# The first routing step handed to the gather in two halves of eight expert numbers

## What is computed

```python
s1 = jnp.einsum('chk,nk->chn', q[..., :128], keys_1)
s2 = jnp.einsum('chk,nk->chn', q[..., 128:], keys_2)
v1, i1 = lax.top_k(s1, 16)
v2, i2 = lax.top_k(s2, 16)
cand = v1[..., :, None] + v2[..., None, :]
cand_idx = i1[..., :, None] * 128 + i2[..., None, :]
top_s, pos = lax.top_k(cand, 16)
experts = take_along_axis(cand_idx, pos)
gate = softmax(top_s)
u, v = expert_u[experts], expert_v[experts]
act = gelu(einsum('chkd,cd->chk', u, h))
out = einsum('chk,chkd->cd', gate * act, v)
```

## Time and profile before

| | us |
|---|---|
| three timed runs | 2411.83, 2418.49, 2420.32; median 2418.49 |
| profiled execution, its own time | 2412.99 |
| its span in the trace | 2411.3 |
| first gather issued at | 920.23 |
| last gather issued at | 2384.3 |

### The profile page before, as it was taken

The page is one execution under the profiler, slowest core; times in us unless marked ns, Lnnn a source line. Parts: engine busy times, 40 slices in busy tenths (PEclk is TensorE's granted clock), DMA queues, the critical chain, the costliest instruction groups (busy, mean ns, idle before and its releaser), DMA issues.

```text
span 2411.3 us, 26498 instructions
## 1 busy us (share of the span) xinstructions
PE 2082.3 (86%) x8832; PEld 1483.9 (62%) x8832; DVE 1679.4 (70%) x3760; ACT 861.5 (36%) x2094; POOL 634.9 (26%) x606
## 2 busy tenths in 40 slices
PE   7999998899999998999986878787788878777776
PEld 3444787788888887877765666676644423322322
DVE  5563645476657737999998999876676666676654
ACT  2321345421103213423326446356643333342332
POOL 2100000000110002333344334344444443444442
PEclk9999998999999999999997989899799999999999
DMA  8631120266774348999999999999999999999997
GB/s 350 197 121 55 34 71 1 105 225 228 259 282 147 133 157 326 412 417 415 418 416 420 407 379 402 399 398 420 420 420 421 421 421 422 419 421 419 421 422 292
DMA packets 131790, 754.31 MB, mean 313 GB/s; under 512 B 14544, under 2 KB 14672, under 8 KB 65616
## 3 DMA queue, kind: packets, MB, share of 16 engines
q0 software_dynamic: 87456, 588.90, 60.0%
q1 hardware_dynamic: 44208, 163.84, 18.7%
HBM read 750.59 MB, written 2.10 MB: 312 GB/s over the span
## 4 chain that ended last, share of the span: by engine, by line
PE 43%; DMA 31%; DVE 16%; ACT 5%; issue 3%; POOL 0%; DVEq 0%; SPq 0%; ACTq 0%; POOLq 0%
PE PS L603 41%; DMA arena<-experts_dram,ecur 25%; DVE arena L2622 5%; DVE arena L1891 4%; DVE h_all L1891 2%; DMA ring<-down_dram 2%; PE PS L1149 2%; DVE ring L1891 1%; DMA ring<-up_dram 1%; DVE arena L1885 1%; ACT L1761 1%; ACT arena L1765 1%; ACT arena L1771 1%; ACT const L1773 1%; DMA ring<-query_dram 1%
## 5 line engine op out<-in xcount | busy, mean ns | idle before, releaser
L603 PE MATMUL PS<-h_all,ring 128*128 128x256 f32 (+2 forms) x3584 | 895.9, 408 | 18.2 <-DMA ring<-up_dram 6.1
L2814 POOL DMA_INDIRECT arena<-experts_dram,ecur x512 | 585.8, 1144 | 1092.7 <-PE PS L1149 385.6
L2622 DVE CUSTOM_DVE_ANT_0 arena<-arena 128x1024 f32<-128x1024 f32 x512 | 626.1, 1223 | 282.8 <-DMA arena<-experts_dram,ecur 279.7
L603 PEld LDWEIGHTS PS<-h_all,ring 128*128 128x128 f32 x3584 | 681.1, 193 | 208.3 <-issue 102.8
L603 PE MATMUL PS<-arena,const 128*128 128x512 f32 (+1 forms) x1056 | 497.0, 618 | 135.7 <-ACT const L1773 125.1
L603 PEld LDWEIGHTS PS<-arena,const 128*128 128x128 f32 x1056 | 198.4, 196 | 418.5 <-issue 220.3
L1149 PE MATMUL PS<-const,arena 128*128 128x128 f32 x1304 | 196.6, 308 | 117.3 <-ACT arena L1771 113.4
L1761 ACT ACTIVATE arena<-arena 128x2 f32<-128x2 f32 x255 | 51.6, 202 | 659.4 <-DVE arena L2622 659.0
L1149 PEld LDWEIGHTS PS<-const,arena 128*128 128x128 f32 x1304 | 171.6, 159 | 143.4 <-ACT arena L1771 125.6
L603 PE MATMUL PS<-arena,ring 128*128 128x256 f32 x1088 | 245.9, 384 | 13.3 <-DMA ring<-down_dram 7.3
L603 PEld LDWEIGHTS PS<-arena,ring 128*128 128x128 f32 x1088 | 205.9, 192 | 47.8 <-DMA ring<-down_dram 12.8
(11 more groups left out here) (279 smaller groups left out, 1659.8 us busy)
## 6 DMA issues: line engine op xcount, KB each, us to landing
ring<-up_dram SPq DMA_DIRECT2D x88, 512.0 KB, 3.4
ring<-w_in_dram SPq DMA_DIRECT2D x80, 512.0 KB, 4.1
arena<-ada_dram POOLq DMA_DIRECT2D x80, 512.0 KB, 5.2
ring<-w_out_dram SPq DMA_DIRECT2D x32, 512.0 KB, 4.9
ring<-query_dram SPq DMA_DIRECT2D x32, 512.0 KB
ring<-down_dram SPq DMA_DIRECT2D x16, 704.0 KB, 5.9
ring<-branch_dram SPq DMA_DIRECT2D x16, 512.0 KB
arena<-experts_dram,ecur POOLq DMA_INDIRECT x512
```

The costliest lines, as they stand in the source:

```text
L603: return nc.tensor.matmul(o, l, r, start=start, stop=stop)
L2622: V.tensor_tensor_reduce(out=u, in0=u, in1=hrow[:, (r // HEADS) % 2, :], scale=1.0, scalar=0.0, op0=MUL, op1=ADD, accum_out=dots[:, p % NB ...
L2814: nc.gpsimd.indirect_dma_start(out=ring_e[:, g % RING, :], out_offset=None, in_=a["experts"], in_offset=bass.IndirectOffsetOnAxis(ap=ecur[ ...
```

## The change

For step 0 alone, the work of stages 11 to 15 is done in two calls of a new function `choose`, each over eight of the 16 positions. The first stands behind stage 7 and writes `ecur[:, 0, 0:8]`; the second stands where stage 15 stood, behind stages 8 to 10. Each increments `ecur_ready`, so that step 0 has two increments, and the number that POOL waits for at each later step is one higher. POOL issues gathers 0 to 7 of step 0 after the first and waits for the second ahead of gather 8. In step 0 the subtraction that gives `gcur` comes behind the second write of `ecur` instead of ahead of it. Steps 1 to 31 keep their code.

```diff
+            def choose(r, lo, hi):
+                settled()
+                V.tensor_scalar(pab[:, 0, lo:hi], pcur[:, lo:hi], 4, None, ALU.logical_shift_right).then_inc(vec_step, 1)
+                V.tensor_scalar(pab[:, 1, lo:hi], pcur[:, lo:hi], 15, None, ALU.bitwise_and).then_inc(vec_step, 1)
+                n(vec_step), n(vec_step)
+                settled()
+                copy(ifl[:, :, lo:hi], pab[:, :, lo:hi]).then_inc(vec_step, 1)
...
+                tt(eqv[:, :, lo:hi], last(ifl[:, :, lo:hi], 16), mid(iota, 2, hi - lo), ALU.is_equal).then_inc(vec_step, 1)
...
+                tt(eqv[:, :, lo:hi], eqv[:, :, lo:hi], idf.unsqueeze(2).to_broadcast([P, 2, hi - lo, 16]), MUL).then_inc(vec_step, 1)
...
+                V.tensor_reduce(sel[:, :, lo:hi], eqv[:, :, lo:hi], X, ADD).then_inc(vec_step, 1)
...
+                stt(exf[:, lo:hi], sel[:, 0, lo:hi], float(NKEYS), sel[:, 1, lo:hi], MUL, ADD).then_inc(vec_step, 1)
+                n(vec_step)
+                settled()
+                copy(ecur[:, r % 2, lo:hi], exf[:, lo:hi]).then_inc(ecur_ready, 1)
...
                 elif j == 7:
                     V.max_index(pcur[:, 0:8], tcur[:, 0:8], cand).then_inc(vec_step, 1)
                     n(vec_step)
+                    if r == 0:
+                        choose(0, 0, 8)
...
+                elif r == 0 and j < 15:
+                    pass
+                elif r == 0:
+                    choose(0, 8, 16)
+                    tt(gcur[:, r % 3, :], tcur, tcur[:, 0:1].to_broadcast([P, 16]), SUB).then_inc(sm_in, 1)
...
             for r in range(STEPS):
-                pool.wait_ge(ecur_ready, r + 1)
+                pool.wait_ge(ecur_ready, r + 2 if r else 1)
                 for j in range(TOPK):
+                    if r == 0 and j == 8:
+                        pool.wait_ge(ecur_ready, 2)
```

## The result

The changed kernel took 2420.32 us (median of 22 runs, 2417.0 to 2432.31), the kernel before 2416.57 us (median of 22 runs, 2411.83 to 2422.21). The ratio is 1.0017, with an interval of 1.0011 to 1.0024: about 4 us slower. That is inside the 0.5% that the forecast called the same, and the time lies in the forecast range, but that range was made wide enough for the spread of the runs, so hitting it says little. The sign is the opposite of the one forecast, and the interval excludes no change. The profiled execution took 2417.3 us, with a span of 2415.6; the forecast for it was 2411.9.

A forecast was written before the change was run, and what follows sets the result against it. From 924 us on, DMA bytes were taken as the bound. Gathers 2.34 us earlier fill 1.1 us of free DMA time, other terms nothing: 2412.99 - 1.1 = 2411.9 profiled, 2415.7 - 1.1 = 2414.6 median, range 2406 to 2426.

The forecast's parts named there:

- the same: Whole kernel: a time within about 0.5%, 12 us, of the kernel before; chance 0.88.
- the sum of rows: Step 0 on DVE: one `choose` on half the columns takes 2.06 us up to the start of its last copy.
- DVE's extra work: Step 0: eight instructions stand twice, 1.55 us, all hidden in DVE's 3.00 us idle time before `route(1, 0)`'s scores.
- The ninth gather: Step 0: POOL reaches it at 927.9, its numbers are there at 921.35, so no added wait, by 6.5 us.
- lock: First gathers: the second `choose` could hold GpSimd's descriptor writing until 921.5; worst 2414.3; in weights late's joint 0.20 chance.
- The sag: 1324 to 1624 us, 16.4 us of DMA time lost: doubled gives 2429.4, chance 0.04; vanished gives 2396.6, chance 0.06.
- The first softmax: Step 0: its input comes 1.7 us later, at 921.5, but ACT reaches it only at 933.77, so no cost.
- The gain at the start: First nine gathers: issued 2.34 us earlier, they fill 1.1 us of free DMA time; bound 1.5 by bytes.
- The step that failed: Tenth gather: its issue stays at 948.10, because the first dot product doesn't move.
- the reserve: Gathers' queue at 948.10: 2.0 to 2.4 us of transfers remain, so it doesn't run dry before the tenth gather.
- Weights late: Before the first dot: gathers slow two weight transfers, +1.0 to +2.0 us, giving 2413 to 2415; joint chance 0.20.
- hidden anyway: Gathers' queue: rows land earlier, but it may run dry at the next thin point; time 2413.0; chance 0.22.

The follow-up runs named there:

- e1: The changed kernel, but POOL waits for both halves of step 0's numbers before its first gather; 2415.55 us against 2416.88 for the kernel before.
- e4: The changed kernel with only two gathers early; the third waits until DVE has finished stage 0 of `route(1, 0)`; 2416.0 us.
- e5: The changed kernel with POOL pausing ahead of its sixth gather for TensorE's report of `query(0, 5)`; 2415.08 us against 2416.02 for the kernel before.
- e15: The changed kernel with a pause ahead of the sixth gather, ended by DVE's counter instead of TensorE's report; 2415.43 us.
- e2: The changed kernel with `expand(2)`, `up_tap(2)` and `expanded(2)` moved beside the first steps; 2411.6 us, ratio 0.9980 to the kernel before.
- e16: A repeat measurement of the changed kernel with `expand(2)` and its followers moved; 2413.62 us against 2416.36 for the kernel before, ratio 0.9992.
- e3: The kernel before, without the split, with `expand(2)`, `up_tap(2)` and `expanded(2)` moved beside the first steps; 2417.37 us, ratio 1.0003.
- e7: The changed kernel with the nine first gathers replaced by direct loads of fixed rows on the same queue; no kernel time given in the text.
- e8: The kernel before with a wait for `query(0, 5)`'s report ahead of the sixth gather, already met when reached; no kernel time given in the text.
- e6: The changed kernel with `expand(2)` and its followers moved and a pause for `query(0, 5)`'s report ahead of the sixth gather; 2413.54 us, ratio 0.9992.

## Why the prediction was wrong, point by point

**Right.** One `choose` took 915.71 to 917.77, 2.06 us, exactly the sum of rows. The first copy came 2.35 us early (2.34 forecast), the second 3.92 us behind it (3.76 forecast; DVE stood idle for 0.30 us ahead of 919.63). DVE's extra work disappeared in the idle time, 1.35 us of which is left (1.45 forecast), and e1 shows its price as nothing. The ninth gather didn't wait for the second half. Gathers issued while the second `choose` ran took 0.98 and 1.00 us, at most the 1.00 of the earlier trace rows and at most 0.06 us more than the second and third gather of the kernel before (0.96 and 0.94): there was no lock. So the Trainium skill's rule in "SBUF — State Buffer" ("SBUF: two separate sides"), weighed in the prediction, isn't seen here either. The sag stayed as it was; by the earlier trace rows it reaches from the 23rd to the 27th slice, not to the 29th. The first softmax had its input in time.

**Mis-sized.** The gain at the start is 0.81 MB or 1.9 us, above the forecast 1.1 and its bound of 1.5. I chose the share of busy time over the bytes; the bytes were nearer. In the early windows the engines' busy time moves less than on the plateau (119 GB/s at a share of 0.45 in the earlier trace rows, where 420 times 0.45 would be 189), so free time by the share understates what more could be moved. With the reports of both queries on time the net of the change can be read against e4, e5 and e15: all three 0.9997, that is -0.7 us, with intervals from about -2.9 to +1.7 us. They hold the forecast -1.1 and also zero. With `expand(2)` out of the way in both kernels, e2 and e16 against e3, it is -5.6 and -2.7 us.

**The step that failed** is this sentence: "It is issued when TensorE has used row 0, at 948.10, and this does not move, since the first dot doesn't." The first dot moved by 4.7 us. The sentence rested on the order in which work depends on work, and no such dependence runs from the gathers to `expand(2)`; the report of TensorE that stands between them was taken to arrive when it is sent. The price was then the reserve that this used up: 2.0 to 2.4 us of gathers were to be left at 948.10, so 4.7 us of delay leave a hole of 2.3 to 2.7 us, or 3.1 with the 1.9 us that were measured. The windows show 4.8 us; a new gather fills the engines only after a while (issued at 953.18, share 0.00 from 952 to 954, 0.58 from 954 to 956, 1.00 from 956), and the prediction's own bound for that, 1.8 us, brings 3.1 to 4.9.

**The rivals.** "Weights late" had the place and the sign, 0.20 chance. Its price, +1.0 to +2.0 us, was taken from longer transfers (9.29 against 8.29), and 2413 to 2415 us came of it for the profiled execution; that took 2417.3. The transfer for `expand(2)` took 8.29 us and was issued 4.9 us late. So it was right by another mechanism than its own. Its own mechanism exists and is smaller: in e5, e7 and e15 one transfer, that for `query(0, 7)`, takes 0.8 to 0.9 us longer and the first dot comes 0.6 to 0.8 us later. Its test, a first dot after 941, and that of "hidden anyway", a share under 0.95 about 948 to 952 (0.07 from 950 on), both came true. "Hidden anyway" ended at no change, and didn't foresee a loss. The warning sign was in the trace of before: the earlier trace rows has ACT reach the first softmax at 933.77, which is only so late because of the hold: the row L1687 at 933.09 ended an idle time of 6.34 us, where those at 922.02 and 925.92 had 3.07. I used the number and didn't ask what had made it.

**Shown, and open.** Shown: the hold of the report sets the issue of `expand(2)`'s weights (two engines see it at once); with a pause both query reports are on time and the loss is gone (e4, e5, e15); with `expand(2)` elsewhere the hold stays and the loss goes (e2, e16). Open is what holds the report. It isn't the kind of semaphore, nor a missing wait, nor bytes alone. The hold was there in 12 of 13 profiles of nine gathers without a pause; the exception is e8, whose kernel showed it in its other profile. With a pause it was there in e4, on a report due 6.55 us into the seven gathers behind the pause, and not in e5, e6 and e15, where no report of the two queries or the key scores falls due so late in a run; nor in e7 with direct loads. In the others a report due 6.1 us after the first gather arrived on time (`key_scores(0, 4)` before the change, ACT's row at 926.36), and one due 8.0 us after it didn't (changed, e1). The held ones came free 0.1 to 2.0 us after the ninth gather's issue had ended. All this fits a hold that begins more than 6.1 us into an unbroken run of gathers, in e4 by 6.55 us, and ends about when the run does; e8 shows that it doesn't always come. Whether it is the count of gathers, their time, or descriptors on their way wasn't told apart.

## What to carry to other kernels

Earlier transfers are worth only what the next link behind them keeps: before moving a burst forward, list every signal that falls due during the burst and ask who needs it at once. An idle time that is longer than those of the same row before it (6.34 us against 3.07) is a question to settle before its number is used. And where a burst must go early, a short pause in it, or moving the one urgent piece out from behind it, can bring back more than the early start did.

## What the runs showed of the hardware

While POOL issues nine gathers 1.25 us apart, TensorE's reports to other engines can arrive late, with TensorE itself on time: 2.1 us in e4 (seven gathers), 3.3 to 5.0 us in the 12 other profiles that show it. They arrive within 2.0 us after the ninth gather's issue. The Trainium skill, "TensorE: Matmul & The Clock Gate" (section "The cost: per-tile semaphore tail"), says that where the matmul of every tile increments a semaphore the increments queue up, some 26 ns for each. No row here shows that number, and the rows of ACT and SP at 931.17 and 931.16 show a delay about 190 times as large, for which that rule has no term.

Beside the gathers the 512 KB weight transfers on these chains took between 8.29 and 9.29 us; for `query(0, 7)` it was 8.29 us with the gathers as before and 9.20 us with the first five of them 2.3 us earlier (e5).
